# A hybrid encoder layer on one core: GpSimd takes the low part of the first expert weights and one plane of the routing gates

## What is computed

```python
pg_all = softmax(t @ w_group + b_group); g = argmax(pg_all); pg = max(pg_all)
el = (t @ w_router + b_router).reshape(-1, N_GROUPS, EXPERTS_PER_GROUP)   # 4 x 4
wv, idx = top_k(softmax(el[of group g]), 2)
wv = wv / sum(wv) * pg                      # the two gates of a token
hid = einsum('td,edf->tef', t, w_up); a, u = split(hid, 2)
act = silu(a) * u * gate
y = einsum('tef,efd->td', act, w_down)
```

## Time and profile before

| | us |
|---|---|
| median of 3 runs (lowest, highest) | 873.52 (872.64, 874.91) |
| the profiled execution, its own time | 872.39 |
| its span in the profile | 870.6 |
| TensorE busy (share of the span) | 796.2 (91%) |
| VectorE busy | 602.4 (69%) |
| ScalarE busy | 350.5 (40%) |
| GpSimd busy | 315.7 (36%) |

### The profile page before, as it was taken

One profiled execution on the slowest core, in us unless ns is written; L12 is line 12 of the kernel. 1 busy time (PEld: TensorE's weight loads), 2 busy tenths in 40 slices (PEclk: granted clock), 3 DMA queues, 4 the chain that ended last, 5 costly groups with the idle time before them and its releaser, 6 DMA issues. The chain is left out here.

```text
span 870.6 us, 13381 instructions
## 1 busy us (share of the span) xinstructions
PE 796.2 (91%) x4773; PEld 624.5 (72%) x4774; DVE 602.4 (69%) x685; ACT 350.5 (40%) x645; POOL 315.7 (36%) x259
## 2 busy tenths in 40 slices
PE   3999999999987999999999995599999999999783
PEld 3689999999944555667767783378888888888431
DVE  6779689742089865776787566998557998571088
ACT  3810111111255663444464434544444544444044
POOL 3000899940000001100000001258665887653056
PEclk9999999999989899999999996699999999999897
DMA  8956544530082501320202038787779998788783
GB/s 323 398 187 209 168 130 139 173 97 2 22 294 82 133 26 49 98 73 25 74 26 73 25 122 273 281 330 279 249 262 349 400 377 292 257 321 286 253 300 140
DMA packets 77362, 165.32 MB, mean 190 GB/s; under 512 B 7397, under 2 KB 32517, under 8 KB 75266
## 3 DMA queue, kind: packets, MB, share of 16 engines
q1 hardware_dynamic: 68402, 132.15, 43.9%
q0 software_dynamic: 7760, 28.31, 9.2%
q10 hardware_dynamic: 1152, 4.19, 1.4%
HBM read 132.57 MB, written 32.08 MB: 189 GB/s over the span
## 5 line engine op out<-in xcount | busy, mean ns | idle before, releaser
L2097 PE MATMUL psum<-we_hi,x_parts 128*128 x384 | 137.4, 403 | 1.6 <-DVE we_lo L1721 1.1
L1721 DVE TENSOR_TENSOR we_lo<-we_raw,we_hi 128x2048 fp32r<-128x2048 f32 x48 | 116.1, 2422 | 1.5
L1720 DVE CAST we_hi<-we_raw 128x2048 fp32r<-128x2048 f32 x44 | 60.4, 1372 | 46.6 <-DMA we_raw<-in_w_down_dram 24.5
L449 PE MATMUL psum<-hn_hi,w_hi 128*128 128x364 f32 (+1 forms) x384 | 90.7, 331 | 1.3 <-issue 0.7
L449 PE MATMUL psum<-hn_lo,w_hi 128*128 128x364 f32 (+1 forms) x384 | 90.1, 329 | 0.0
L449 PE MATMUL psum<-hn_hi,w_lo 128*128 128x364 f32 (+1 forms) x384 | 89.9, 328 | 0.0
L2097 PEld LDWEIGHTS psum<-we_hi,x_parts 128*128 128x128 f32 x384 | 72.2, 188 | 16.7 <-issue 2.4
L1040 PE MATMUL psum<-wo_hi,mixin 128*128 128x512 f32 (+1 forms) x256 | 83.4, 397 | 0.0
L2097 PE MATMUL psum<-we_lo,x_parts 128*128 x192 | 75.2, 392 | 0.0
L633 DVE SCALAR_TENSOR_TENSOR proj<-wm,cT,proj 128x2048 f32<-128x2048 f32 x28 | 74.1, 2694 | 1.0 <-DMA wm<-in_w_mod_dram 1.0
L449 PEld LDWEIGHTS psum<-hn_hi,w_hi 128*128 128x128 f32 x384 | 67.0, 189 | 5.7 <-issue 4.9
(11 more groups left out here) (331 smaller groups left out, 1595.3 us busy)
## 6 DMA issues: line engine op xcount, KB each, us to landing
we_raw<-in_w_up_dram SPq DMA_DIRECT2D x32, 1024.0 KB, 8.4
wm<-in_w_mod_dram SPq DMA_DIRECT2D x16, 1024.0 KB, 5.1
we_raw<-in_w_down_dram SPq DMA_DIRECT2D x16, 1024.0 KB, 6.2
w_raw<-in_w_in_dram SPq DMA_DIRECT2D x16, 512.0 KB, 6.3
we_raw<-ff_d SPq DMA_DIRECT2D x12, 512.0 KB, 6.6
proj<-in_x_prompt_dram SPq DMA_DIRECT2D x4, 1024.0 KB, 8.1
sc_room<-in_w_mod_dram SPq DMA_DIRECT2D x4, 1024.0 KB, 14.2
proj<-in_w_mod_dram SPq DMA_DIRECT2D x2, 2048.0 KB, 12.0
```

Of the source, the lines that this page charges most:

```text
L449: mm = pe.matmul(psum[:, 3 * slot + c, 0:n], w[:, slot, k, :], hn[:, k, t0:t0 + n], start=(k == 0 and w is w_hi and hn is hn_hi), stop=(k ...
L1720: then(dve.tensor_copy(we_hi[:, a:b], raw))
L1721: dve.tensor_tensor(we_lo[:, a:b], raw, we_hi[:, a:b].bitcast(F32), ALU.subtract).then_inc(ready, 1)
L2097: mm = pe.matmul(psum[:, bank, :], x[:, s, k, :], w[:, bass.ds(at + k * 2 * DE, 2 * DE)], start=(k == 0 and x is x_hi and w is we_hi), sto ...
```

## The change

`cmp` gets a tile of its own. The reduction to `texpf` moves from ahead of `where` and `ids` to behind them. GpSimd, ahead of its wait for the first rows' names, waits for the first half of expert 0's up matrix and for ScalarE's high part and computes the low part; VectorE's `split(0, 0)` becomes a wait for `up_ready` 1. Plane 2 of ont, the one with the gates' first part, goes from VectorE to GpSimd, behind plane 5 and ahead of the third gather; the first `gate_parts` copy signals `r_shift` 4 for it, and TensorE's second by_slot waits for `r_const` 7 rather than 6.

```diff
--- before.py
+++ after.py
@@ -1472,7 +1472,7 @@
         out_ids = sb("out_ids", [P, TC], I32)
         ont = sb("ont", [P, TILES, 2, 7, TC], BF16)
         onf = ont[:, :, :, 6, :]
-        cmp = xg[:, 0, 0:TC * NE].rearrange("p (t e) -> p t e", e=NE)
+        cmp = sb("cmp", [P, TC, NE])[:, :, :]
         gslot = sb("gslot", [P, TC])
         texpf = sb("texpf", [P, TC])
 
@@ -1684,13 +1684,12 @@
 
             then(dve.tensor_tensor(cmp, cum[:, None, :].broadcast_to([P, TC, NE]),
                                    tstart[:, :, None].broadcast_to([P, TC, NE]), ALU.is_le))
-            then(dve.tensor_reduce(texpf[:, :], cmp, AX_X, ALU.add))
-
             dve.wait_ge(r_counts, 2)
             then(dve.tensor_copy(where[:, :], psum[:, 6, 0:TC]))
             dve.scalar_tensor_tensor(out=ids[:, :], in0=psum[:, 6, TC:2 * TC], scalar=spare_row[:, 0:1], in1=where[:, :],
                                      op0=ALU.add, op1=ALU.add).then_inc(ids_ready, 1)
 
+            then(dve.tensor_reduce(texpf[:, :], cmp, AX_X, ALU.add))
             dve.tensor_scalar(cumi[:, :], cum[:, :], 1.0 / P, 1.0, ALU.mult, ALU.add)
             dve.tensor_scalar(ntile[:, :], cum[:, NE - 1:NE], 1.0 / P, 1.0, ALU.mult, ALU.add)
             then(dve.tensor_scalar(texp[:, :], texpf[:, :], float(NE - 1), None, ALU.min))
@@ -1731,14 +1730,18 @@
             then(dve.reciprocal(gates[:, :, 0:1], l1[:, :, :]))
             then(dve.tensor_tensor(gates[:, :, 1:2], gates[:, :, 0:1], l2[:, :, :], ALU.mult))
             for n in range(3):
-                then(dve.tensor_copy(gate_parts[n][:, :, :], gates[:, :, :]))
+                if n == 0:
+                    dve.tensor_copy(gate_parts[0][:, :, :], gates[:, :, :]).then_inc(r_shift, 1)
+                    dve.wait_ge(r_shift, 4)
+                else:
+                    then(dve.tensor_copy(gate_parts[n][:, :, :], gates[:, :, :]))
                 if n < 2:
                     then(dve.tensor_tensor(gates[:, :, :], gates[:, :, :], gate_parts[n][:, :, :], ALU.subtract))
-            for n in range(3):
+            for n in range(1, 3):
                 last = dve.tensor_tensor(ont[:, :, :, 2 + n, :], onf, gate_parts[n][:, :, :, None].broadcast_to(full + [TC]), ALU.mult)
             last.then_inc(oneh_ready, 1)
 
-            split(0, 0)
+            dve.wait_ge(up_ready, 1)
             split(0, 1)
             split(0, 2)
             dve.wait_ge(r_counts, 3)
@@ -1797,6 +1800,9 @@
                 pool.dma_start(ff_d[at:at + P, :].rearrange("p (k n) -> p k n", n=P),
                                spare[:, None, :].broadcast_to([P, KC, P])).then_inc(scattered[half], 16)
             pool.memset(one_row[:, :], 1.0).then_inc(r_const, 1)
+            pool.wait_ge(up_loaded[0][0], 16)
+            pool.wait_ge(first_hi, 1)
+            pool.tensor_tensor(we_lo[:, 0:UP // 2], we_raw[:, 0:UP // 2], we_hi[:, 0:UP // 2].bitcast(F32), ALU.subtract).then_inc(up_ready, 1)
             pool.wait_ge(scattered[0], 16)
             pool.wait_ge(scattered[1], 16)
             pool.wait_ge(ids_ready, 1)
@@ -1831,6 +1837,8 @@
             pool.tensor_scalar(upshift[:, :, :], upper[:, :, :], float(FF_ROWS), 0.0, ALU.mult, ALU.add).then_inc(r_const, 1)
             pool.wait_ge(r_const, 5)
             pool.tensor_tensor(ont[:, :, :, 5, :], onf, upshift[:, :, :, None].broadcast_to(full + [TC]), ALU.mult).then_inc(r_const, 1)
+            pool.wait_ge(r_shift, 4)
+            pool.tensor_tensor(ont[:, :, :, 2, :], onf, gate_parts[0][:, :, :, None].broadcast_to(full + [TC]), ALU.mult).then_inc(r_const, 1)
             fetch_first(2, 2)
             fetch_first(3, 3)
             gate_act(0, None)
@@ -2135,7 +2143,7 @@
             lower_first(0)
             lower_first(1)
             pe.wait_ge(oneh_ready, 3)
-            pe.wait_ge(r_const, 6)
+            pe.wait_ge(r_const, 7)
             by_slot(7, 2, 6, False)
             first, second = places(1)
             up(0, 0, first, None, step0, FIRST_BANK)
```

## The result

The changed kernel takes 875.78 us (median of 20 runs, 873.21 to 882.78), the one before 872.79 us in 20 runs beside it. The ratio is 1.0038, with a 95% interval of 1.0022 to 1.0055: slower, by 3.3 us (872.79 x 0.0038; 1.9 to 4.8 by the interval). The profiled execution has a span of 872.9 us against 870.6.

What follows compares the result with a forecast made beforehand. TensorE is never idle in the expert stage, so the routing chain, mostly on VectorE, sets the end; 4.5 + 0.15 + 0.9 - 0.8 - 0.95 = +3.8 us on 873.1 gives 876.9 us, range 874.7 to 878.9.

Steps and rivals of the forecast that it cites:

- the shorter hold: Rival: GpSimd starts after sel, or runs at the 1.89 us addition's rate; each gives +2.9 us, both +2.0; chance 0.25.
- 1 first hold: Routing: GpSimd's 2048-element subtraction holds VectorE's sel until it is over, +4.5 us.
- 2 where waits for TensorE: Routing: with texpf moved back, VectorE stands for TensorE's by_slot(6) before where, +0.15 us.
- 3 second holds: Gates: GpSimd's existing plane holds L1732 (-0.1) and its new plane holds the second cast (+1.0), together +0.9 us.
- 4 plane taken off: Gates: VectorE does one of three planes less, -0.8 us.
- 5 by_slot(7) ends the wait: Before the first expert matmul: by_slot(7) and the tile-table reading, 1.6 us, replace 2.55 us by way of split(0, 0), -0.95 us.
- GpSimd is in first: Routing: GpSimd's subtraction starts at 546.9, before VectorE's sel, due at 546.98, so sel is held.
- The rate of the 1.89 us addition: First hold, lower bound: from a 1023-element GpSimd addition, the subtraction takes 3.8 us and delays by 3.6 us.
- The rival without a hold: GpSimd's long instruction lets VectorE through at sel, and the new plane costs nothing; sum -1.6 us, 871.5; chance 0.08.
- The longer hold: Rival: GpSimd's subtraction takes 5.5 us, or its two short planes follow each other; +4.6 to +5 us, 878; chance 0.09.
- no effect of the earlier rows on the end: Start of the expert stage: naming and gathering the first rows earlier is worth nothing at the end.
- The clock: TensorE between warm-up and expert matmuls: granted in full (1.00, 2.4 GHz), effect taken as 0.

Runs made afterwards that it cites:

- left_out: The changed kernel without GpSimd's subtraction, ScalarE writing zeros for the first low part; 871.87 us, ratio 0.9988 to the kernel before.
- early: The kernel before with ids ahead of texpf, first low part ahead of the gates, tile 0's up product ahead of by_slot(7); 869.96 us, ratio 0.9975.
- the second profile: The changed kernel, unaltered, run and profiled once more; median 876.88 us, ratio 1.0045 to the kernel before.
- plane_alone: The kernel before with only the first gate plane moved from VectorE to GpSimd; ratio 1.0004, routing 27.05 us.
- early2: The version early with TensorE reading the tile table ahead of turning the first rows; 871.54 us, ratio 0.9987 to the kernel before.

## Why the prediction was right, and where it was not

The direction, the mechanism and, roughly, the size held: a hold on VectorE until GpSimd's instruction is over, 876.9 us forecast and 875.78 measured, within the range of 874.7 to 878.9. The whole time (slower by 1.9 to 4.8 us) cannot tell the forecast's +3.8 us from the +2.9 us of the shorter hold; the steps in the profile can:

| step | forecast | measured | from |
|---|---|---|---|
| 1 first hold | +4.5 | +3.7 | cast 3.87 for 0.18; changed less left_out, 3.63 |
| 2 where waits for TensorE | +0.15 | +0.25 | 0.27 idle before L1688, 0.02 usual |
| 3 second holds | +0.9 | +0.84 | L1731 +0.92, L1737 +0.96, less the 1.04 of before |
| 4 plane taken off | -0.8 | -0.74 | 1.58 for 2.32 |
| 5 by_slot(7) ends the wait | -0.95 | -0.96 | 567.33 to 568.92, 1.59 for 2.55 |
| sum | +3.8 | +3.1 (routing: +3.0) | |

**The step that failed** is in the first: "GpSimd is in first". I gave ScalarE's signal 0.07 us to reach GpSimd; it took 0.16 (546.80 to 546.96). The profile before also had the weights 5.58 us after L1630, where the later ones had them at 5.70 to 5.97. Sel therefore always went first, and 0.8 us of VectorE's work passed under the hold. This is the rival of the shorter hold (+2.9), to which I gave 0.25 against the forecast's 0.58, and the measured +3.1 is its case. Both of its terms, the signal and the arrival of the weights, were taken too short. By the prediction's own numbers (546.9 against sel at 546.98) 0.1 us too late was enough, not the 0.3 that it names in step 1. What I called a matter of 0.1 us of arrival was not a matter of chance. The rate of the 1.89 us addition, its other half, did not come: 2048 elements took 4.52 to 4.65 us, a little under two of the 2.36 us instructions. The Trainium skill's 4497 ns (GPSIMD Engine Reference, section 3.1) is 0.02 to 0.15 us below that.

Step 2 was short by 0.1 us because by_slot(6) ends at 558.19 and where starts at 558.30; the prediction gave this handing over nothing.

The rival without a hold is excluded by every run with a GpSimd instruction in that place. Its sum of -1.6 left out the second hold as well; left_out, with that hold still in, gives -0.6. The longer hold did not come either. The forecast of no effect of the earlier rows on the end held as long as split(0, 0) or by_slot(7) released TensorE; in early the x parts made from those rows release it. The clock, which I took at 0, was 1.00 from 564 us on in the changed kernel. Before that, in the warm-up, it was still 0.52 at 562 to 564 us and the warm-up took 6.57 us (5.72 in the second profile, 5.87 in the kernel before); by_slot(7) stood 0.57 us for VectorE all the same (0.94 in the second profile), so this did not reach the first expert matmul. plane_alone shows that the clock can cost 1.3 us at this place. Step 3 came within 0.1 us: in both kernels each short GpSimd instruction meets one VectorE instruction, as reckoned.

## What to carry to other kernels

Idle time of GpSimd beside a VectorE that is on the chain is not free: beside a GpSimd instruction that reads SBUF, VectorE pays for what is left of it as soon as it comes to a cast, a small tensor_scalar or an instruction with two SBUF tensors (3.6 of 4.65 us here), and cutting it in pieces returns little (0.5 of 3.6 us). Before work is moved off the chain, ask also what becomes the next release: here 2.2 us taken off were worth 1.0, since TensorE's own by_slot(7) stood behind. Moving what is not needed yet (by_slot(7) behind the first product, the gates behind the low part) shortened the routing by 1.9 us where the offload lengthened it by 3.0; in the whole time it gave 0.25% in early and nothing measurable in early2, where the offload cost 0.38%.

## What was not expected of the hardware

A GpSimd memset of 1.8 us, which reads nothing, holds a VectorE cast and a tensor_scalar of 18 elements (1.83 us for 0.18) like a subtraction does. The way from ScalarE's end to the start of GpSimd's subtraction was 0.15 to 0.16 us, against the 0.02 to 0.03 us between VectorE's own dependent instructions. And the granted clock fell just after the warm-up in one profile (0.50 from 566.5 to 569.5 us in plane_alone) and stayed at 1.00 in that of the kernel before, with as much idle time ahead.
